# Merge tile 0 prepared inside the delta stage, logits moved inside a projection, expert gathers moved behind a stage border

## The chip, the cores and the metric

One core of one Trainium2 chip. The metric is the device time of one execution in microseconds. Engines are named as in the profile: PE (TensorE matmul), DVE (VectorE), ACT (ScalarE), POOL (GpSimd), SP (SyncE, which here only issues DMAs). Each engine runs its own list of instructions in order and waits on semaphores for the others.

## The reference

One layer of a bidirectional encoder over 1024 sample tokens and 256 prompt tokens, D = 1024, all in float32:

```python
x += W_out( sig(gA) * W_pA(GatedDeltaNet_bidir(n)) + sig(gB) * W_pB(DilatedWindowAttn(n)) )   # n = RMSNorm(x)
x += ExpertChoiceSwiGLU(RMSNorm(x))
# merge of the mixer, per token:
oa = rmsnorm(o_fwd + o_bwd, a_norm) * silu(z)              # 8 heads of 64
ya = oa @ w_proj_a
weights = softmax(stack(lses)); ob = sum(weights * outs)   # 3 dilation groups, 4 heads
yb = ob @ w_proj_b
x = x + (sigmoid(gate_a) * ya + sigmoid(gate_b) * yb) @ w_out
# routing: every expert takes its best tokens (128 of the sample, 32 of the prompt)
aff = softmax(rmsnorm(x) @ w_router); gate, idx = top_k(aff.T, cap)
ye = (silu(x[idx] @ w_gate) * (x[idx] @ w_up)) @ w_down * gate     # added back at idx; 16 experts
```

## The kernel before

The layer is a chain of stages, each a Block in which all five engines run their lists. A Block ends when every engine has drained; then the stage's semaphores are cleared and a second barrier lets the next stage begin (signals, L48).

phase_delta (L1419) walks 20 chunks of 64 tokens (STEPS), 16 of the sample and 4 of the prompt. Both directions go side by side: the backward half of step s works on the last chunk not yet done, so that tokens 0 to 127 are complete once the sample's 16 steps are stored. In each step PE solves and carries, ACT copies u and w (L1638, L1639), then the state and the outputs (L1641, L1644), DVE masks and carries (L1655 to L1675), POOL prepares later steps (L1498 to L1505). SP loads step s and stores step s-3; at step 16 it also issues the mixer's weights (load_mixer, L1725: w_proj_a, w_proj_b and w_out in two halves) into the buffer "weights", whose eight slots later hold expert weights (HELD = 8).

phase_merge (L1770) takes 10 tiles of 128 tokens (8 sample, 2 prompt). For a tile POOL adds the two directions, squares, scales and multiplies by silu(z) (L1894 to L1904); DVE sums the squares and prepares the softmax over the three groups (statistics, L2110) and mixes them (weighted, L2122, result mg_ob); ACT does Silu, Sigmoid, Ln, Exp with a table load at each change (L2062 to L2073). PE turns the two inputs (turn_in), projects them in two column halves (project_in, 12 matmuls each), DVE multiplies with the gates (gated, L2096), PE turns the mix (turn_mix), projects it (project_out, 16 records per half), DVE adds x (residual), ACT finds the root (L2053 to L2057), DVE scales (normed), PE turns and finds the logits (turn_normed, logits), ACT and DVE make affinities, PE turns them (turn_affinities), DVE keeps them (take_affinities). The tiles are staggered by a hand-written order over c = 0 .. 14: PE in iteration c does project_in of tile c-2, turn_mix and project_out of c-3, turn_normed and logits of c-4, turn_affinities of c-5, turn_in of c-1 (L1988 to L2013).

Routing ranks affinities eight at a time on DVE, 16 rounds over the 640 tokens of tiles 0 to 4 (low_best), 16 over the rest (high_best, 384 wide; the last four rounds also rank the prompt). A fixed number of rounds is placed between the other work: LOW_AT_ONCE (L1745) inside the loop over c, and the list from L2234 behind it. The two lists are merged, PE turns the indices, DVE writes them to the tensors of Routing (L1748), and POOL gathers the first inputs of the experts (L1905 to L1909) before the Block ends. keep_busy (L562) issues matmuls with the identity whose results nobody reads.

phase_experts (L2302) turns the gathered rows, splits them in a rounded part and a rest, and multiplies 12 weight pieces per expert for 16 experts: multiply(e, n).

## Time and profile before

| | us |
|---|---|
| median of three runs (2550.56 to 2558.72) | 2550.92 |
| profiled execution | 2563.21 |
| its span, first to last instruction | 2561.5 |
| last delta matmul ends | 1321.9 |
| merge's first load is issued | 1327.33 |
| first merge transpose | 1353.47 |
| merge's Block ends | 1681.5 |
| first expert product | 1695.31 |
| mean granted clock of TensorE, share of full speed | 0.966 |

Times inside the execution are microseconds from the start of the span. The profile is of one execution, so sums are made against 2563.21.

### The profile page before, as it was taken

How to read it: one execution, taken by the hardware profiler on the slowest of the kernel's cores; microseconds unless marked ns; L12 is line 12 of the kernel's file. 1: busy time of each engine (PE TensorE's matmuls, PEld its weight loads, DVE VectorE, ACT ScalarE, POOL GpSimd, SP SyncE). 2: the span in 40 equal slices, each digit the busy share in tenths (PEclk: the TensorE clock that was granted, in tenths of full speed). 3: DMA queues.
4: the chain of work that ended last, by engine and by line, in shares of the span. 5: the costliest groups of instructions: out<-in, count | busy, mean ns of one | idle time of the engine just before them, and what ended most of it. 6: DMA issues, size and time to landing. Idle time of an engine off the chain costs nothing. (4 is left out here: it accounts for less than half of the span.)

```text
span 2561.5 us, 49483 instructions
## 1 busy us (share of the span) xinstructions
PE 2366.1 (92%) x20746; PEld 2117.0 (83%) x20746; DVE 1389.6 (54%) x1774; ACT 1079.3 (42%) x1605; POOL 394.4 (15%) x411
## 2 busy tenths in 40 slices
PE   6988899889999999988868999979999999999996
PEld 5766688889999988988853555579999999999996
DVE  5544411134444367332226456867777777777776
ACT  4555511111111068111126553246666666666664
POOL 1000000000000094644313220000000100010001
PEclk8999999999999999998988999989999999999998
DMA  3333432238666377444644441448777877777765
GB/s 118 76 86 86 108 117 95 97 102 264 184 203 185 131 216 220 129 127 122 216 123 149 134 139 55 184 173 282 267 248 274 269 264 274 263 261 263 274 233 195
DMA packets 174174, 461.30 MB, mean 180 GB/s; under 512 B 57361, under 2 KB 103057, under 8 KB 146353
## 3 DMA queue, kind: packets, MB, share of 16 engines
q1 hardware_dynamic: 160944, 412.63, 49.2%
q0 software_dynamic: 13024, 45.70, 6.2%
q8 instruction: 158, 2.59, 0.4%
q14 instruction: 48, 0.39, 0.0%
HBM read 359.94 MB, written 102.24 MB: 180 GB/s over the span
## 5 line engine op out<-in xcount | busy, mean ns | idle before, releaser
L78 DVE TENSOR_TENSOR ex_w_rest<-weights,ex_w_rounded 128x2048 fp32r<-128x2048 f32 x192 | 439.5, 2290 | 209.8 <-ACT ex_w_rounded L2531 208.0
L2531 ACT CAST ex_w_rounded<-weights 128x2048 fp32r<-128x2048 f32 x192 | 365.6, 1905 | 25.9 <-PEq L48 25.9
L2422 PE MATMUL ex_u_acc<-ex_xt,ex_w_rounded 128*128 128x320 f32 x1024 | 271.7, 348 | 0.0
L2422 PE MATMUL ex_g_acc<-ex_xt,ex_w_rounded 128*128 128x320 f32 x1024 | 270.1, 347 | 1.6 <-issue 1.6
L85 PE MATMUL tk_acc<-tk_w_rounded,normed 128*128 128x336 f32 x800 | 257.3, 322 | 6.8 <-DVE tk_w_rest L78 6.8
L85 PE MATMUL tk_acc<-tk_w_rounded,normed_rest 128*128 128x336 f32 x800 | 255.0, 319 | 0.0
L85 PE MATMUL tk_acc<-tk_w_rest,normed 128*128 128x336 f32 x800 | 254.6, 318 | 0.0
L2423 PE MATMUL ex_u_acc<-ex_xt,ex_w_rest 128*128 128x160 f32 x1024 | 242.1, 236 | 0.0
L2423 PE MATMUL ex_g_acc<-ex_xt,ex_w_rest 128*128 128x160 f32 x1024 | 242.0, 236 | 0.0
L2423 PEld LDWEIGHTS ex_u_acc<-ex_xt,ex_w_rest 128*128 128x128 f32 x1024 | 196.4, 192 | 0.0
L2423 PEld LDWEIGHTS ex_g_acc<-ex_xt,ex_w_rest 128*128 128x128 f32 x1024 | 196.3, 192 | 0.0
L2422 PEld LDWEIGHTS ex_g_acc<-ex_xt,ex_w_rounded 128*128 128x128 f32 x1024 | 192.9, 188 | 1.8 <-issue 1.8
L2422 PEld LDWEIGHTS ex_u_acc<-ex_xt,ex_w_rounded 128*128 128x128 f32 x1024 | 193.0, 189 | 0.2
L85 PEld LDWEIGHTS tk_acc<-tk_w_rounded,normed 128*128 128x128 f32 x800 | 152.0, 190 | 10.5 <-DVE tk_w_rest L78 7.0
L85 PE MATMUL ch_wide<-normed,ch_w_rounded 128*128 128x512 f32 x384 | 152.0, 396 | 5.2 <-DMA ch_headsum<-in_headsum 5.2
L1177 DVE COPY tk_stage<-tk_acc 128x336 f32<-128x336 f32 x50 | 25.4, 508 | 241.8 <-PE tk_acc L85 241.8
L1116 ACT COPY tk_stage<-tk_acc 128x336 f32<-128x336 f32 x50 | 21.8, 437 | 313.8 <-PE tk_acc L85 313.8
L85 PEld LDWEIGHTS tk_acc<-tk_w_rest,normed 128*128 128x128 f32 x800 | 152.1, 190 | 0.0
L85 PEld LDWEIGHTS tk_acc<-tk_w_rounded,normed_rest 128*128 128x128 f32 x800 | 151.5, 189 | 0.0
L85 PE MATMUL ch_wide<-normed_rest,ch_w_rounded 128*128 128x512 f32 x384 | 150.7, 392 | 0.0
L85 PE MATMUL ch_wide<-normed,ch_w_rest 128*128 128x512 f32 x384 | 150.6, 392 | 0.0
L1945 PE MATMUL mg_out<-weights,mg_mix_t 128*128 128x512 f32 x320 | 141.4, 595 | 0.3 <-ACT mg_mix_t L2041 0.3
(342 smaller groups left out, 5239.4 us busy)
## 6 DMA issues: line engine op xcount, KB each, us to landing
weights<-in_w_expert SPq DMA_DIRECT2D x192, 1024.0 KB, 5.0
laq<-sc_laq SPq DMA_DIRECT2D x20, 768.0 KB, 4.0
dl_la<-laq SPq DMA_DIRECT2D x20, 768.0 KB, 5.2
proj_tok<-tk_stage SPq DMA_DIRECT2D x9, 1680.0 KB, 7.8
tk_w<-in_w_tok SPq DMA_DIRECT2D x10, 1344.0 KB, 6.8
ch_w<-in_w_ch SPq DMA_DIRECT2D x24, 512.0 KB, 4.1
sc_rows<-rows SPq DMA_DIRECT2D x40, 256.0 KB, 6.5
sc_qk<-qkv_ch SPq DMA_DIRECT2D x40, 256.0 KB, 6.8
```

Of the source, the lines that this page charges most:

```text
L78: return dve.tensor_tensor(out, whole, rounded.bitcast(F32), ALU.subtract)
L85: mm = pe.matmul(out, stationary[a], moving[b], start=(first and n == 0), stop=(last and n == len(pairs) - 1))
L1116: act.copy(stage[:, c % 2, t, :], acc[:, n % BANKS, 0:TOK_BLOCK]).then_inc(copied[0], 1)
L1177: dve.tensor_copy(stage[:, c % 2, t, :], acc[:, n % BANKS, 0:TOK_BLOCK]).then_inc(copied[1], 1)
L1945: mm = pe.matmul(out[:, h, :], mix_t[:, k, :], wo[k // 4][:, k % 4, h * 512:(h + 1) * 512], start=(k == 0), stop=(k == KT - 1))
L2422: pe.matmul(bank[:, 0:2 * SLOTS], hi[:, cols], x.rearrange("p a n -> p (a n)"), start=first, stop=False, skip_group_check=True)
L2423: return pe.matmul(bank[:, 0:SLOTS], lo[:, cols], x[:, 0, :], start=False, stop=last, skip_group_check=True)
L2531: act.copy(w_hi[:, i % SPLIT], held[:, i % HELD]).then_inc(w_rounded, 1)
```

## The change

- A class FirstTile holds tile 0 of the merge. It is loaded by SP in the delta stage, before the store of step 16, into slots 3, 6 and 7 of "weights". POOL's sums and scale, ACT's Silu, roots and Sigmoid, DVE's statistics and weighted of tile 0 stand in the delta stage's lists around the last step; PE gets 16 keep_busy matmuls at its end.
- The second half of w_out, which had slots 6 and 7, is loaded at the start of the merge behind tile 1's inputs, under a semaphore of its own (rest_ready), on which project_out(0, 0) waits. MIXER_WEIGHTS is 3.
- The merge's engines count up tile 0's semaphores (sem_inc) and start with tile 1. The constants are loaded at c = 1; nobody waits for them at the start.
- PE's order for the first tiles is written out, and so is the iteration of the last sample tile.
- DVE's ranking rounds and tail are placed anew; the last tile's turned mix goes to a free gates buffer.
- The two first gathers are issued by POOL at the start of the expert stage; the sample's comes first there, and the prompt's turn writes to y_acc. BUSY_RANKS is 16 instead of 30, BUSY_GATHER 12 instead of 20.

```diff
@@ phase_delta, SP
+                    if isinstance(s, int) and s == STEPS - 1:
+                        for r in range(2):
+                            sp.wait_ge(stored[r], 32 * S_STEPS // 2)
+                        first_tile.load(sp, io, dr)
@@ phase_delta, POOL, PE, ACT, DVE
                 ring_steps(pool, prepare)
+                first_tile.sums(pool)
+                first_tile.scale(pool)
                 ring_steps(pe, step)
+                keep_busy(pe, ybank[:, 0, 0:P], ident, 16)
                 def step(s, b, i, prompt):
+                    if isinstance(s, int) and s == STEPS - 1:
+                        first_tile.activate(act)
                     act.wait_ge(uw_done, s + 1)
...
                     act.copy(paired(wb[:]), uw[:, :, :, 1, :]).then_inc(uw_out, 1)
+                    if isinstance(s, int) and s == STEPS - 1:
+                        first_tile.roots(act)
...
                 ring_steps(act, step)
+                first_tile.open_gates(act)
...
+                    else:
+                        first_tile.statistics(dve)
                     carried(s, b)
...
                 ring_steps(dve, step)
+                first_tile.weighted(dve)
@@ FirstTile (new; six loads on one semaphore)
+    def load(self, sp, io, dr):
+        rows = slice(0, P)
+        for d in range(2):
+            sp.dma_start(self.od[:, d], dr["o_delta"][d, rows, :]).then_inc(self.loaded, 16)
+        sp.dma_start(self.z, dr["proj_tok"][rows, Z_AT:Z_AT + HEADS * HD]).then_inc(self.loaded, 16)
+        sp.dma_start(self.att.rearrange("p g c -> p (g c)"), dr["att_out"][rows, :]).then_inc(self.loaded, 16)
+        sp.dma_start(self.gates, dr["proj_tok"][rows, GATE_AT:GATE_AT + 2 * D]).then_inc(self.loaded, 16)
+        sp.dma_start(self.again[:], io["a_norm"].partition_broadcast(P)).then_inc(self.loaded, 16)
+    def sums(self, pool):       # add the directions, square
+    def scale(self, pool):      # times rstd, a_norm, silu(z); waits rstd, then silu
+    def activate(self, act):    # waits loaded; Silu of z
+    def roots(self, act):       # waits mean, eps; Ln, Exp; waits dm; Exp
+    def open_gates(self, act):  # Sigmoid of the gates
+    def statistics(self, dve):  # waits squared; head sums, maxima
+    def weighted(self, dve):    # waits exp; weights, three products, reduction to ob
@@ phase_merge, SP
-                load(0)
-                for dst, src in ((again...), (fgain...), (wr...)):
-                    sp.dma_start(dst, src).then_inc(S["const"], 16)
+                sp.sem_inc(inputs[0], 64)
+                sp.sem_inc(gates_in[0], 16)
+                load(1)
+                load_rest(sp)
                 for c in range(NT + LAST):
-                    if has(c + 1):
+                    if c >= 1 and has(c + 1):
                         load(c + 1)
+                    if c == 1:
+                        for dst, src in ((fgain...), (wr...)):
+                            sp.dma_start(dst, src).then_inc(S["const"], 16)
@@ phase_merge, POOL
-                for b in range(2):
-                    pool.wait_ge(hn_stored[b], 16 * NT // 2)
-                pool.wait_ge(S["handed"], 2)
-                routing.gather_prompt(pool, dr, 0)
-                routing.gather(pool, dr, 0)
@@ phase_merge, PE
-                for c in range(NT + LAST):
+                turn_in(0)
+                project_in(0, 0)
+                project_in(0, 1)
+                turn_mix(0)
+                project_out(0, 0)
+                turn_in(1)
+                project_out(0, 1)
+                project_in(1, 0)
+                project_in(1, 1)
+                turn_in(2)
+                for c in range(4, NT + LAST):
...
+                    if c - 4 == LAST_SAMPLE:
+                        turn_normed(c - 4)
+                        project_out(c - 3, 0, range(KT // 2))
+                        pe.wait_ge(S["aff_taken"], c - 4)
+                        logits(c - 4)
+                        project_out(c - 3, 0, range(KT // 2, KT))
+                        turn_affinities(c - 4)
+                        turn_mix(c - 2)
+                        project_out(c - 3, 1)
+                        continue
@@ phase_merge, ACT: turned_out(0) first; in c = 1 after the roots of tile 1
+                    if c == 1:
+                        mix_out(0)
+                        open_gates(1)
@@ phase_merge, DVE
-LOW_AT_ONCE = {9: (0, 1, 2), 10: (1, 2, 3), 11: (1, 2, 3)}
+LOW_AT_ONCE = {9: (0, 0, 1, 2), 10: (1, 1, 2, 3)}      # the first number stands between highest and normed
+                gated(0, 0)
+                gated(0, 1)
+                for c in range(1, NT + 1):                # gated(c - 2) only from c = 3
...
+                highest(LAST_SAMPLE - 1)
+                low_best(1)
+                normed(LAST_SAMPLE)
+                affinities(LAST_SAMPLE - 1)
+                gated(NT - 1, 0)
+                low_best(1)
+                gated(NT - 1, 1)
+                take_affinities(LAST_SAMPLE - 1)
+                low_best(2)
+                highest(LAST_SAMPLE)
+                affinities(LAST_SAMPLE)
+                low_best(1)
+                take_affinities(LAST_SAMPLE)
+                residual(NT - 2, 0)
+                high_best(3)
+                residual(NT - 2, 1)
                 high_best(2)
                 normed(NT - 2)
+                residual(NT - 1, 0)
                 low_best(ROUNDS - low_rounds[0])
-                residual(NT - 1, 0)
                 high_best(4)
                 residual(NT - 1, 1)
                 high_best(1)
                 highest(NT - 2)
                 normed(NT - 1)
                 affinities(NT - 2)
+                high_best(2)
                 take_affinities(NT - 2)
-                high_best(1)
                 highest(NT - 1)
-                high_best(1)
                 affinities(NT - 1)
@@ phase_experts
+                gather(0)            # POOL, first in its list
+                gather_prompt(0)
                 keep_busy(pe, g_acc[:, 0, 0:P], ident, BUSY_GATHER)
+                turn_in(0)
                 turn_in_prompt(0)
-                pe.wait_ge(xpt_lo, 2)
-                turn_in(0)
@@ ACT and DVE of phase_experts: round_x(0), rest_x(0) stand before the prompt's
```

## Rows read from the trace of the kernel before

**Rows 1.** The page, part 1: busy time, share of the span, instructions.
```profile
PE 2366.1 (92%) x20746; PEld 2117.0 (83%) x20746; DVE 1389.6 (54%) x1774; ACT 1079.3 (42%) x1605; POOL 394.4 (15%) x411
```

**Rows 2.** Waits, 1321 to 1358: who <- whom: total us, times, longest.
```profile
PE mg_in_turned L1964 <- DVE mg_ob L2139: 31.5, 1, 31.5
POOL mg_on L1894 <- DMA mg_wr<-in_w_router: 11.7, 1, 11.7
```

**Rows 3.** Timeline of PE: start, us, instructions [idle before <-releaser].
```profile
1356.74 5.76 PE L1923 MATMUL mg_y<-weights,mg_mixin_t 128*128 128x512 f32 x8 [1.76 <-ACT mg_mixin_t L2084]
...
1370.91 3.70 PE L1923 MATMUL mg_y<-weights,mg_mixin_t 128*128 128x512 f32 x8 [0.89 <-ACT mg_mixin_t L2084]
...
1376.16 1.04 PE L1936 MATMUL mg_wide_turned<-identity,mg_mix 128*128 128x128 f32 x8
...
1382.81 7.03 PE L1945 MATMUL mg_out<-weights,mg_mix_t 128*128 128x512 f32 x16
...
1397.20 3.60 PE L1923 MATMUL mg_y<-weights,mg_mixin_t 128*128 128x512 f32 x8
...
1404.37 3.70 PE L1923 MATMUL mg_y<-weights,mg_mixin_t 128*128 128x512 f32 x8 [0.99 <-DVE mg_mix L2103]
...
1426.59 3.68 PE L1923 MATMUL mg_y<-weights,mg_mixin_t 128*128 128x512 f32 x8
```

**Rows 4.** Timelines of ACT and DVE at the merge's start.
```profile
1334.83 1.28 ACT L2065 ACT_TABLE_LOAD   x1 [11.76 <-DMA mg_att<-att_out]
...
1341.40 1.91 ACT L2067 ACTIVATE mg_gates<-mg_gates 128x2048 f32<-128x2048 f32 x1
...
1348.98 3.27 DVE L2134 TENSOR_TENSOR mg_wv<-mg_att,mg_st 128x256 f32<-128x256 f32 x3
...
1373.76 1.94 DVE L2134 TENSOR_TENSOR mg_wv<-mg_att,mg_st 128x256 f32<-128x256 f32 x3
```

**Rows 5.** Timeline of DVE at the merge's end.
```profile
1637.21 0.54 DVE L2199 MAX8 mg_high_val<-mg_high_aff 16x8 f32<-16x384 f32 x1
...
1644.32 0.69 DVE L2149 TENSOR_TENSOR mg_x<-mg_out,mg_x 128x512 f32<-128x512 f32 x1
...
1653.92 0.28 DVE L2179 COPY mg_high_aff<-mg_in_turned 16x128 f32<-16x128 f32 x1 [4.23 <-PE mg_in_turned L1983]
...
1664.31 0.55 DVE L2199 MAX8 mg_high_val<-mg_high_aff 48x8 f32<-48x384 f32 x1
```

**Rows 6.** Drains at the merge's end (ns, start); the prompt gather's landing.
```profile
L1836 DVEq DRAIN  x1: 415/415/415, 1673.6 to 1673.6; - x1
L1836 POOLq DRAIN  x1: 6634/6634/6634, 1674.9 to 1674.9; - x1
...
DMA to landing us min/median/max: 4.3/4.3/4.3
```

**Rows 7.** Timeline of PE at the expert stage's start; one window behind it.
```profile
1682.63 7.54 PE L562 MATMUL ex_g_acc<-identity 128*128 128x128 f32 x40 [9.10 <-PEq L48]
...
1695.31 0.50 PE L2422 MATMUL ex_g_acc<-ex_xt,ex_w_rounded 128*128 128x320 f32 x1 [1.61 <-issue]
...
1700.00:1750.00 50.00, 50.00 (x393) 50.00 (x392) 38.27 (x36) 33.27 (x36) 2.20 (x2) 1.00 0.81 298
```

**Rows 8.** Timelines of ACT and DVE, from x2 to the scaled tile.
```profile
1598.36 1.06 ACT L2053 ACTIVATE mg_sqx<-mg_x 128x1024 f32<-128x1024 f32 x1 [6.61 <-DVE mg_x L2149]
...
1602.67 1.29 DVE L2157 SCALAR_TENSOR_TENSOR mg_hn<-mg_x,mg_st,mg_fgain 128x1024 f32<-128x1024 f32 x1 [3.05 <-ACT mg_st L2057]
```

**Rows 9.** DMA queues, 1326 to 1345.
```profile
DMA packets 2769, 5.11 MB, mean 269 GB/s; under 512 B 1360, under 2 KB 1360, under 8 KB 2512
```

**Rows 10.** Delta steps: waits of PE 1236 to 1280; ACT's copy of u.
```profile
PE dl_sbank L1602 <- issue: 3.0, 2, 1.6
...
1266.54 0.58 ACT L1638 COPY dl_u<-dl_ubank 128x512 f32<-128x512 f32 x1 [6.55 <-PE dl_ubank L1526]
...
1315.12 0.58 ACT L1638 COPY dl_u<-dl_ubank 128x512 f32<-128x512 f32 x1 [2.62 <-PE dl_ubank L1526]
```

More of the change, by code:

```diff
@@ L1712 @@
 HALF = 512
-MIXER_WEIGHTS = 4
+MIXER_WEIGHTS = 3
 def shared_weights(nc, ctx, io):
@@ L1726, in load_mixer, with load_mixer_rest @@
         rows = lambda w: w.rearrange("(k p) c -> p k c", p=P)
-        for dst, src in ((mixer[0], rows(io["w_proj_a"])), (mixer[1], rows(io["w_proj_b"])),
-                         (mixer[2][0], rows(io["w_out"])[:, 0:4]), (mixer[2][1], rows(io["w_out"])[:, 4:])):
+        for dst, src in ((mixer[0], rows(io["w_proj_a"])), (mixer[1], rows(io["w_proj_b"])), (mixer[2][0], rows(io["w_out"])[:, 0:4])):
             engine.dma_start(dst, src).then_inc(mixer_ready, 16)
+    def load_mixer_rest(engine):
+        engine.dma_start(mixer[2][1], io["w_out"].rearrange("(k p) c -> p k c", p=P)[:, 4:]).then_inc(mixer_rest_ready, 16)
     def load_expert(engine, pieces):
@@ L1821, in phase_merge @@
         listed, prompt_listed = y[:, 0, :], out[:, 0, :]
+        last_mix_t = gates[:, (NT - 3) % 3, 0:D].rearrange("p (k n) -> p k n", k=KT)
+        gate = lambda t: gates[:, t % 3] if t else first_tile.gates
+        mixes_t = lambda t: last_mix_t if t == NT - 1 else mix_t
         S = {n: sem(f"mg_{n}") for n in (
@@ L1937, in turn_mix, with project_out @@
                     mm.then_inc(S["mix_turned"], 1)
-                def project_out(t, h):
+                def project_out(t, h, ks=range(KT)):
                     if h == 0:
@@ L1943, in project_out @@
                         pe.wait_ge(S["x2"], 2 * (t - 1) + h + 1)
-                    for k in range(KT):
-                        mm = pe.matmul(out[:, h, :], mix_t[:, k, :], wo[k // 4][:, k % 4, h * 512:(h + 1) * 512], start=(k == 0), stop=(k == KT - 1))
-                    mm.then_inc(S["out_done"], 1)
+                    else:
+                        pe.wait_ge(rest_ready, 16)
+                    for k in ks:
+                        mm = pe.matmul(out[:, h, :], mixes_t(t)[:, k, :], wo[k // 4][:, k % 4, h * 512:(h + 1) * 512], start=(k == 0), stop=(k == KT - 1))
+                    if ks.stop == KT:
+                        mm.then_inc(S["out_done"], 1)
                 def turn_normed(t):
                     pe.wait_ge(S["hn"], t + 1)
-                    pe.wait_ge(S["mix_t"], min(t + 2, NT))
+                    pe.wait_ge(S["mix_t"], min(t + 2, NT) if t != NT - 2 else NT)
                     for k in range(KT):
@@ L1972, in logits @@
                         pe.wait_ge(S["lexp"], t)
+                    else:
+                        pe.wait_ge(S["const"], 32)
                     pe.wait_ge(S["on_t"], min(t + 4, NT))
@@ L2215, in _ @@
                         affinities(c - 5)
-                    if has(c - 2):
+                    if has(c - 2) and c > 2:
                         gated(c - 2, 0)
@@ L2220, in _ @@
                     low_best(low_a)
-                    if has(c - 2):
+                    if has(c - 2) and c > 2:
                         gated(c - 2, 1)
@@ L2549, in round_prompt @@
                             act.wait_ge(xt_prompt, GANG * g)
-                        act.copy(xpt[:, 4 * half:4 * half + 4, 0, :], turned[:, half].rearrange("p (k n) -> p k n", k=4)).then_inc(xpt_hi, 1)
+                        act.copy(xpt[:, 4 * half:4 * half + 4, 0, :], prompts_turned(g)[:, half].rearrange("p (k n) -> p k n", k=4)).then_inc(xpt_hi, 1)
                 def gate_half(e, j):
@@ L2670, in rest_prompt @@
                         here = xpt[:, 4 * half:4 * half + 4]
-                        rest(dve, here[:, :, 1, :], turned[:, half].rearrange("p (k n) -> p k n", k=4), here[:, :, 0, :]).then_inc(xpt_lo, 1)
+                        rest(dve, here[:, :, 1, :], prompts_turned(g)[:, half].rearrange("p (k n) -> p k n", k=4), here[:, :, 0, :]).then_inc(xpt_lo, 1)
                 def gate_sum(e, j):
```

257 lines of the change are left out of this document (164 added, 93 removed).

## The prediction

> **What bounds the kernel now.** I read the page first: TensorE (PE) is busy for 92% of the span [rows 1], so time can come only from stretches in which PE waits, or from work taken off the path. Three such stretches lie where the diff works.
>
> First, the list of waits around the border of the delta rule and the merge: PE waits 31.5 us for the first tile's attention mix, mg_ob [rows 2]. In order of time: the last delta matmul ends at 1321.9 and the merge's first loads are issued at 1327.33 (both in the table); ScalarE (ACT) is released by the inputs' landing at 1334.83, the first add on GpSimd (POOL) waits 11.7 us for the router weights, and the first transpose comes 31.5 us after the last delta matmul, at 1353.47 [rows 2, 4].
>
> Second, the end of the merge. From tile 3 on (project_in at 1426.59 [rows 3]) PE runs on without a gap, so there only its own work counts. Then the ranking on VectorE (DVE) is what is late: it idles 4.23 us for the turned affinities at 1653.92, and its last four rounds start only at 1664.31 [rows 5].
>
> Third, the entry of the expert stage: POOL's drain at the merge's end takes 6634 ns, from 1674.9 to 1681.5, while DVE's took 415 ns at 1673.6; PE then starts at 1682.63, fills 7.54 us with 20 keep_busy matmuls, turns two inputs from about 1690, and multiplies from 1695.31 [rows 6, 7]. After that PE is full to the end (50.00 of 50 us, clock 1.00) [rows 7], so what is gained before 1695.31 is gained in the total.
>
> **Part 1: the merge starts with tile 0 prepared.** I write times on the old axis. Inside the delta stage: POOL has done its last preparation at 1295, so the sum and square of tile 0 (1.3 + 1.0 us) cost nothing; ACT loads a table and does Silu in the 2.6 us before the last step's copies; the two root tables and DVE's 1.4 us of statistics fit into waits of 5.8 and 5.2 us. After the last carry (1319.5) DVE has 1.0+0.2+0.2+0.9, three products (3.27 us beside POOL, 1.94 alone [rows 4]) and a 1.0 reduction: done at 1325.5 to 1326.3. ACT's Sigmoid of the gates follows the last output copy at 1323.1: table 1.28 + 1.91 [rows 4] = 1326.3. The last stores end the stage at 1326.2 now, so I put the stage's end 0.9 later and the first transpose at 1328.2.
>
> From there I walk PE's new order with the old pitches [rows 3]: a copy gap 0.9, project_in pairs 10.5 (2 x 5.25, from 1370.91 to 1376.16), mixed 1.8 later, turn 0.9, project_out half 6.9 (7.03 with its overlap). Up to turn_mix(0) this gives 1343.3. But ACT must first finish tile 1's roots, whose sums DVE takes only after gated(0,1) at 1342.2; 0.7 + 0.3 + table 1.28 + 0.4 bring the copy of the mix to 1345.0 and project_out(0,0) to 1346.1. Then: half 1353.0, turn 1353.7, half 1360.6, project_in of tile 1 1371.1, turn 1371.8, project_in(2,0) 1372.7. Old was 1397.20, so 24.5 us so far.
>
> There a new wait comes. project_in(2,1) needs gated(2,0), and DVE comes to it only after gated(1,1) (1372.7), weighted(3) (6.2 us beside POOL), two residual halves (1.3), the ACT chain from x2 to the root (1598.36 to the scaling at 1602.67, 4.3 [rows 8]), that scaling (1.3) and the product (0.6): 1386.6. Old was 1404.37 [rows 3]: 17.8 us are left, PE idle 7.6. Such an idle stretch costs clock: after the old one 8 matmuls took 5.76 us at the 1.2 GHz level against 3.70 later [rows 3], 2.1 us; with the smaller gaps before it I take off 3.3. **Part 1: 14.5 us.** Bounds: 24.5 if the chain is not late; 8 if w_out's second half, now loaded after the border, is late too. That load: 4.34 MB stand in the queue up to its end, and the queue moved 5.11 MB at 269 GB/s from 1326 to 1345 [rows 9], so it lands near 1342, 4 us before 1346.1. Queued behind it on SP are tile 2's inputs and the constants, which nobody wants before 1351.
>
> Moves inside the delta stage: 2 MB fewer of mixer weights at 1236, 2.2 MB of tile 0 more at about 1285. With the DMA full, steps stretched: at 1266.54 ACT waited 6.55 us for PE's solve, at 1315.12, undisturbed, 2.62, and PE itself had waits that the profile explains by nothing, 3.0 us in the largest group [rows 10]. Call it 7 to 10 us for the burst of 7 MB, 1.2 us per MB (an estimate from these rows): 2.5 saved, 2.6 paid. I take 0, bounds -5 and +4.
>
> The Trainium skill (Runtime: NRT & Kernel Launch, Instruction fetch mechanics) says that sequential fetch is mostly hidden. By that rule both terms would be nil and the sum the same; the rows speak against it while the DMA is full [rows 10].
>
> **Part 2: the merge's tail.** PE's order is changed (logits of tile 7 inside project_out of tile 8, turn_mix(9) earlier, tile 9's mix in its own buffer), the sum of its work is not; the 0.7 us of gaps at 1628 goes. DVE: three waits of some 3 us take one low round each (2.55). The price: between the residual halves of tile 9 stand now 1 low + 4 high rounds, 2.55 + 7.1 (1637.21 to 1644.32, four rounds and little else [rows 5]) from 1636.0, so the second half comes at 1645.7 instead of 1644.32, 1.3 late, and the norm, turn and logits of tile 9 with it. The gain: all 12 high rounds that need no prompt are done before the turned affinities at about 1655.2, where 7 were, and two of them fill the 4.23 us. What follows is take 0.3, highest 0.3, exponent and affinities 1.3, turn 0.5, take 0.3: the last four rounds start at 1657.8 instead of 1664.31. **Part 2: 6.5 us**, bounds 3 (another slip of the chain through tile 9) and 8 (none). The cut of the keep_busy matmuls (30 to 16) lies beside the four rounds of 7 us and cost nothing unless the clock falls.
>
> **Part 3: gathers after the border.** Before, POOL issued both gathers at the merge's end and its drain held all engines until they had landed [rows 6]: the overlap with the border was none. Now DVE's drain ends it: 1674.0 + 1.1 (1681.5 to 1682.6, as old) = 1675.1. Sample gather from there: 0.9 issue, landed about 5 us after its start, 1680.2 (prompt gather's landing 4.3 us [rows 6]); the prompt's 1.3 later, 1681.6. PE's 12 keep_busy matmuls end by 1679.8. Turn 1.0, prompt turn ending 1682.6, then round, rest and take: 3.3 after the prompt's turn starts, 1685.0 (old: 5.1 from the first turn to the product, the second turn and its round between). Old 1695.31 [rows 7]. **Part 3: 10.3 us**; bounds 12.5 and 6 (a gather that lands 4 us later, beside the first expert weights).
>
> A second rule stands beside parts 1 and 3. The trace has three products at 3.27 us while POOL runs and 1.94 when it does not [rows 4]. The Trainium skill (SBUF — State Buffer, SBUF: two separate sides) calls the port pair of VectorE and GpSimd an exclusive lock for instructions with two SBUF inputs. By it weighted beside POOL's scale ends up to 1.3 us later, which moves the stage's end by less than 1.
>
> Sum: 14.5 + 0 + 6.5 + 10.3 = 31. The profiled execution took 2563.2 us (span 2561.5 and 1.7 around it), so it would be 2532; the median of the runs is 2550.9, 12.3 lower, and I take the same 31 off it: **2520 us**.
>
> **Rivals.**
> (A) *No late chain at the start.* If gated(2,0) is reached in time, because PE's own gaps pull apart less than I walked, part 1 is 24.5 less 1: 2511. For it: old, DVE was only 0.99 us late at this very place; against it: the residuals stand behind weighted(3) in DVE's list, and po(0,1) is now 12 us earlier relative to them without helping.
> (B) *Early loads are paid in delta steps.* Tile 0's 2.2 MB meet steps 17 and 18, and each loses what the half step at 1266 lost, 3.9 us [rows 10], one of them twice that; the saving at 1236 does not come back. With 8 paid, 23: 2528.
> (C) *Gathers or chain slips.* Part 3 gives 6, part 2 gives 3: 2527 or 2528.
> (D) *The other side: w_out's second half.* PE's project_out(0,0) waits for it and everything queues behind. Up to 1346.1 it is free; from there each us costs one. With the 31 us it decides from a landing at 1377. The 4.34 MB would need 87 GB/s, and 8 MB with tile 2's inputs shared in would need 160; the queue gave 269. At 1386 it would give 2560.
> (E) *The change does not do what it says*: tile 0's loads wait for sample stores and land after 1313, so ACT holds the last delta step for them; the gap moves into the stage. Stores of step 15 are issued at 1277.7, 35 us earlier. It would leave parts 2 and 3 alone: 2534.
>
> **How the numbers follow.** Forecast 57%, A 13%, B 11%, C 11%, D 3%, E 5%. The range takes A and C and most of B and E: 2508 to 2535. A measurement of this kernel tells 0.3% (7.7 us) from no change. Faster needs more than 7.7 of the 31: 95%; same 3%, slower 2%, both from D and from tails of B and E together.
>
> **What would show it.** Right: first merge transpose 5 to 7 us after the last delta matmul; POOL's drain at the merge's end under 1 us; a PE wait of 5 to 9 us before project_in(2,1), released by DVE's mix product, and none after it; the last four ranking rounds 6 to 7 us sooner after tile 9's project_in; first expert product about 11 us after DVE's last index copy instead of 21.3. Wrong: PE waiting for a DMA before project_out(0,0), delta steps over 14 us after the loads, or a gather that PE waits for beyond 7 us.

## The result, and the profile after

The changed kernel takes **2534.4 us** (median of 7 runs, 2521.8 to 2538.2); the kernel before took 2558.7 us in its 7 runs of the same comparison (2550.6 to 2569.3). Ratio 0.9908, 95% interval 0.9885 to 0.9930: **24 us faster, between 18 and 29**. The forecast was 31 us, 1.2% of 2550.9. Its sign held, and its range (2508 to 2535) by 0.6 us; the size did not: 1.2% lies outside the interval. Of the 14 us between 2520 and 2534, 7.8 come from the median it started from (2550.9 in three runs, 2558.7 in seven), the rest from the gain.

The profiled execution of the changed kernel happens to be its fastest, 2521.8 us (span 2520.1); 41 us lie between the two profiles, far more than between the medians. So the comparison needs a point that the change can't move. I take ScalarE's last copy of u in the delta rule (1315.12 before [rows 10], 1300.27 after) and count from there; what lies ahead of it is a section of its own below.

| from the last copy of u, us | before | after | gain | forecast |
|---|---|---|---|---|
| to project_in(3,0) (part 1) | 111.47 | 98.53 | 12.9 | 14.5 |
| from there to project_in(9,0) (steady) | 172.48 | 172.47 | 0 | 0 |
| from there to the last four rounds (part 2) | 65.24 | 58.04 | 7.2 | 6.5 |
| from there to the last index copy's end | 9.67 | 9.67 | 0 | 0 |
| from there to the first expert product (part 3) | 21.33 | 15.63 | 5.7 | 10.3 |
| to the first product in all | 380.2 | 354.3 | 25.9 | 31.3 |
| from the first product to the end | 866.2 | 865.5 | 0.7 | 0 |

The delta steps in front of that point cost about 1.2 us more (below, a mean that scatters by over 1 us), which leaves 24.7 of 25.9, near the measured 24. Busy time answers to [rows 1]; PE has 19 us less, in an execution with a mean granted clock of 0.979 against 0.966:

```profile
PE 2347.0 (93%) x20734; PEld 2101.8 (83%) x20734; DVE 1388.1 (55%) x1774; ACT 1079.6 (43%) x1605; POOL 395.2 (16%) x411
```

**Part 1.** The timeline of PE at the merge's start (start, us, instructions, idle before and its releaser), which answers to [rows 2, 3]:

```profile
1313.30 0.63 PE L2071 MATMUL mg_in_turned<-identity,ft_on 128*128 128x128 f32 x4 [2.44 <-DVEq L2228]
...
1315.04 5.22 PE L2027 MATMUL mg_y<-weights,mg_mixin_t 128*128 128x512 f32 x8 [0.89 <-ACT mg_mixin_t L2180]
...
1332.28 8.56 PE L2051 MATMUL mg_out<-weights,mg_mix_t 128*128 128x512 f32 x16 [2.48 <-ACT mg_mix_t L2170]
...
1373.65 6.62 PE L2027 MATMUL mg_y<-weights,mg_mixin_t 128*128 128x512 f32 x8 [7.15 <-DVE mg_mix L2242]
...
1398.80 3.68 PE L2027 MATMUL mg_y<-weights,mg_mixin_t 128*128 128x512 f32 x8
```

The 31.5 us wait is gone: the first transpose comes 6.2 us after the last delta matmul (end at 1307.1; forecast 6.3). The late chain is there as well: PE idles 7.15 us before project_in(2,1) (forecast 7.6), released by VectorE's mix product, and VectorE shows why, since that product stands behind the scaling of tile 0, which waited 4.34 us for ScalarE's root:

```profile
1371.71 1.28 DVE L2298 SCALAR_TENSOR_TENSOR mg_hn<-mg_x,ft_st,mg_fgain 128x1024 f32<-128x1024 f32 x1 [4.34 <-ACT ft_st L2194]
1372.91 0.68 DVE L2242 TENSOR_TENSOR mg_mix<-mg_y,mg_gates 128x512 f32<-128x512 f32 x1
```

What the forecast had too small is the clock: behind each of the three idle stretches (2.44 + 0.89 us around the first turns, 1.58 + 2.48 around the turn of the mix, 7.15) PE's matmuls are slow, 5.22 instead of 3.65 us, 8.56 instead of 7.03 and 6.62 instead of 3.60. That is 6.1 us where 3.3 were taken off. The price of one stretch is not fixed: in the second profile of the same kernel (below) the three groups took 6.65, 8.83 and 5.51 us behind the same waits.

**Part 2.** VectorE at the merge's end [rows 5]: the wait for the turned affinities (second line) is 0.92 us instead of 4.23.

```profile
1617.30 0.69 DVE L2288 TENSOR_TENSOR mg_x<-mg_out,mg_x 128x512 f32<-128x512 f32 x1
...
1626.97 0.28 DVE L2322 COPY mg_high_aff<-mg_in_turned 16x128 f32<-16x128 f32 x1 [0.92 <-PE mg_in_turned L2092]
...
1629.31 0.55 DVE L2342 MAX8 mg_high_val<-mg_high_aff 48x8 f32<-48x384 f32 x1
```

**Part 3.** The drain that took 6634 ns [rows 6] lies now in the middle of the merge (GpSimd's at 1531.9, 1644 ns where under 1 us was forecast; nothing waits for it there); VectorE's ends the stage at 1639.0, and PE starts at 1640.11. Up to there all is as forecast. Then, on the axis of the changed kernel, one timeline per engine:

```profile
1640.81 1.06 POOL L2547 DMA_INDIRECT ex_xs<-hn,rt_sample_idx  x1 [107.33 <-POOLq L48]
1642.18 2.96 POOL L2552 DMA_INDIRECT ex_xp<-hn,rt_gang_idx  x1 [0.30 <-issue]
...
1642.01 2.29 DVE L78 TENSOR_TENSOR ex_w_rest<-weights,ex_w_rounded 128x2048 fp32r<-128x2048 f32 x1 [3.03 <-ACT ex_w_rounded L2694]
...
1644.33 0.33 SPq L2529 DMA_DIRECT2D weights<-in_w_expert  x1
...
1645.36 1.29 PE L2631 MATMUL ex_turned<-identity,ex_xs 128*128 128x128 f32 x8
1650.50 1.97 PE L2639 MATMUL ex_y_acc<-identity,ex_xp 128*128 128x128 f32 x8 [3.86 <-DMA ex_xp<-hn,rt_gang_idx]
1654.61 0.60 PE L2586 MATMUL ex_g_acc<-ex_xt,ex_w_rounded 128*128 128x320 f32 x1 [2.14 <-ACT ex_xt L2706]
```

Read the second gather first: 2.96 us on GpSimd, where both gathers of the kernel before took about 1.0. It is the only one beside which VectorE works on a product with two large inputs in SBUF (the first weight rest, what is left of a weight after rounding); that product began 0.17 us before the gather and ended 0.84 us before the gather did. When that product is done SyncE sends the first weight load (1 MB) off, still ahead of the gather's data. The next gather, at 1646.91, ran beside VectorE's rests of the turned rows, which have one input in PSUM, and took 0.94 us. The prompt is turned 11.5 us after the index copy (forecast 7.6), and the products start at the low clock: the last slow one ends 20.6 us after the copy.

### The profile page after: what moved, and what is told of

Same layout as the page of the kernel before. It is cut to its first block and busy times, and to the rows that moved or that the text cites. A ratio compares the mean times of both kernels' runs of the same rounds, so it can differ in the third digit from the quotient of the medians.

```text
span 2520.1 us, 49483 instructions
## 1 busy us (share of the span) xinstructions
PE 2347.0 (93%) x20734; PEld 2101.8 (83%) x20734; DVE 1388.1 (55%) x1774; ACT 1079.6 (43%) x1605; POOL 395.2 (16%) x411
## 5 line engine op out<-in xcount | busy, mean ns | idle before, releaser
L2586 PE MATMUL ex_y_acc<-ex_ht,ex_w_rounded 128*128 128x320 f32 x512 | 135.1, 347 | 0.2 <-DVE ex_ht L78 0.2
```

The source lines that it names most:

```text
L2586: pe.matmul(bank[:, 0:2 * SLOTS], hi[:, cols], x.rearrange("p a n -> p (a n)"), start=first, stop=False, skip_group_check=True)
```

## The experiments

Times below count from the last copy of u, or, at the expert stage's entry, from the end of the last index copy. The totals are against the kernel before on the same chip.

**Undo one part, or do one alone.** The kernel before with part 3 alone (the expert stage and the gathers from the changed kernel, its 12 keep_busy matmuls):

> Kernel before with part 3 alone: gathers issued in the expert stage, sample first, 12 instead of 20 keep_busy matmuls, turns and rounds in the changed kernel's order. Theory (part 3 is worth what the trace of the changed kernel shows, 5.7 us, and not the 10.3 forecast): from VectorE's last index copy to the first product 15 to 16 us instead of 21.3; total 0.2% less. Rival (the forecast's size was right and the changed kernel's entry was a bad draw): 11 to 12 us, total 0.4% less.

Measured: 2556.4 us, ratio 0.9986 (0.9970 to 1.0002). First product at 15.78, second gather 2.96 us, prompt turned at 11.67. The theory holds for the stretch: part 3 is worth 5.6 us of it by itself, with the same late prompt, so not a bad draw and not a consequence of parts 1 and 2. The total alone would not tell it from nothing.

Two things the 5.6 us hide. The old entry scatters too: in the next run, which leaves it as it was, the first product comes at 19.92 instead of 21.33, so the gain lies between 4.1 and 5.6 us. And in the old entry PE turned the first input right behind its 20 keep_busy matmuls, which took 7.54 us in one profile [rows 7] and 6.21 in the other, though the prompt's gather had landed at 1679.0, 4.3 us after its start [rows 6]:

```profile
1690.01 1.04 PE L2475 MATMUL ex_turned<-identity,rt_xp 128*128 128x128 f32 x8
```

```profile
1675.37 6.21 PE L562 MATMUL ex_g_acc<-identity 128*128 128x128 f32 x40 [9.03 <-PEq L48]
```

So a part of the gain is the cut from 20 to 12 keep_busy matmuls: 8 of 20 are 2.5 to 3.0 us, an estimate from these two groups. No run makes that cut alone.

The kernel before with the second half of w_out loaded at the merge's start:

> Kernel before with one part of the change alone: the second half of w_out (2 MB) is loaded at the merge's start, behind the inputs of tiles 0 and 1, not in the delta rule. Theory of the forecast (2.5 us of stretched delta steps saved): from the copy of step 14 to that of step 19 65 to 66 us instead of 67.4 to 68.2; the rest unchanged, from the last delta copy to the end 1241 to 1246 us. Rival 1 (those steps are not stretched by the load): 67 to 68. Rival 2 (the load at the border delays what the merge's start needs): first merge transpose later than 38.4 us after the last delta copy.

Measured: step 14 to step 19 took 67.1 us, against 68.2 and 67.4 in the two other kernels with the old delta rule; first transpose at 37.6. Rival 1 holds: 2 MB fewer there give nothing that stands out of the scatter. Nor does the load hurt at the border. In the eleven profiles with the new delta rule the same five steps took 67.1 to 70.1, mean 68.8 against 67.6 before; the step after tile 0's loads is 1.5 to 2.0 us longer in ten of them and 0.7 in one, and PE shows a wait of "issue" in it, that is for nothing that the profile shows (waits of PE, 1274.8 to 1288.3 of the changed kernel), while from 1272 to 1276 the DMA engines were full (share 1.03, 407 GB/s):

```profile
PE dl_sbank L1556 <- issue: 1.3, 1, 1.3
```

What PE waited for there no run shows.

Logits of tile 7 behind the whole half of project_out instead of inside it:

```diff
-                        project_out(c - 3, 0, range(KT // 2))
+                        project_out(c - 3, 0)
                         pe.wait_ge(S["aff_taken"], c - 4)
                         logits(c - 4)
-                        project_out(c - 3, 0, range(KT // 2, KT))
```

> Changed kernel with the logits of tile 7 after the whole half of project_out(8,0) instead of inside it. From project_in(9,0) to the last four ranking rounds it is 58.04 us in the changed kernel. Theory (VectorE is full between tile 7's logits and those rounds but for waits of 1.5 and 1.0 us, so logits 3.4 us later come through in part): 59 to 60 us. Rival (the ranks are bound elsewhere, by the residual of tile 9 and its norm chain): 58.0 us, and the move inside is worth nothing.

Measured: 62.33 us instead of 58.04. More than the 3.4 us of the move came through (4.3), so my theory's damping by 1.5 and 1.0 us of waits was wrong; the order inside the projection carries 4.3 of part 2's 7.2 us.

**The late chain.** In VectorE's order at the merge's start:

```diff
+                    if c == 3:
+                        residual(0, 0)
+                        residual(0, 1)
+                        gated(2, 0)
                     if has(c):
                         weighted(c)
```

(and all three left out where they stood)

> Changed kernel with VectorE's order altered at the merge's start only: the residual halves of tile 0 and the mix product gated(2,0) come ahead of weighted(3). Theory (the 7.15 us wait before project_in(2,1) is VectorE's order, and the 6.62 us instead of 3.60 after it is the clock paid for that wait): the wait goes (under 0.5 us), project_in(2,1) takes 3.6 to 3.7 us, and from the merge's first load to project_in(3,0) it is 76 to 77 us instead of 86.4; total about 10 us less than the changed kernel. Rival 1 (the wait moves on: project_out(1,0) or the turning of hn(0) waits for ScalarE's roots instead): 3 to 7 us of it come back in the next 20 us. Rival 2 (the slow matmuls come from the stage's start, not from this wait): the wait goes but project_in(2,1) stays above 5 us.

Measured: 2519.3 us, ratio 0.9849 (0.9827 to 0.9872); project_in(3,0) at 89.79 instead of 98.53 to 99.2 (77.7 from the merge's first load, expected 76 to 77). PE has no wait between turn_mix(1) and project_in(2,1) any more, and the matmuls behind run at full speed:

```profile
1372.81 1.04 PE L2040 MATMUL mg_wide_turned<-identity,mg_mix 128*128 128x128 f32 x8
1373.68 3.60 PE L2027 MATMUL mg_y<-weights,mg_mixin_t 128*128 128x512 f32 x8
```

Theory confirmed, rival 1 and rival 2 both gone: the wait was an order in a list, and 3.0 us behind it were its price in clock.

**The clock at the start.** On top of that kernel: 32 keep_busy matmuls after the delta rule, 6 before project_out(0,0), and ScalarE's copy of mix(0) ahead of tile 1's roots:

```diff
-                keep_busy(pe, ybank[:, 0, 0:P], ident, 16)
+                keep_busy(pe, ybank[:, 0, 0:P], ident, 32)
...
                 turn_mix(0)
+                keep_busy(pe, out[:, 0, 0:P], ident, 6)
                 project_out(0, 0)
```

> The kernel with gated(2,0) ahead, and at the merge's start: 32 instead of 16 keep_busy matmuls at the end of the delta rule, ScalarE's copy of mix(0) ahead of tile 1's roots, 6 keep_busy matmuls between turn_mix(0) and project_out(0,0). Counted from ScalarE's last dl_u copy, that kernel had the first transpose at 13.0 us, project_in(0,0) for 6.12 us from 15.2, project_out(0,0) for 8.83 us from 33.3 and project_in(3,0) at 89.8. Theory (PE's short waits cost clock, and the copy stands behind roots that nobody needs so early): project_in(0,0) 3.6 to 4.5 us, project_out(0,0) from 30.5 for 7.0 us, project_in(3,0) at 84 to 85, 5 us less in total. Rival 1 (the low clock comes from the border's idle itself, not from a short one): project_in(0,0) stays above 5 us, 3 us less in total. Rival 2 (tile 1's roots, now 1 us later, hold turn_in(1) and the copy of its sums): project_out(0,1) and project_in(1,0) a microsecond later, gain of the copy given back.

Measured: 2527.4 us, ratio 0.9867 (0.9829 to 0.9906); project_in(3,0) at 89.93, nothing gained. Two things took the gain:

```profile
1319.56 7.41 PE L562 MATMUL dl_ybank<-identity 128*128 128x128 f32 x64
...
1328.83 0.63 PE L2071 MATMUL mg_in_turned<-identity,ft_on 128*128 128x128 f32 x4 [1.86 <-DVEq L2230]
...
1330.57 3.70 PE L2027 MATMUL mg_y<-weights,mg_mixin_t 128*128 128x512 f32 x8 [0.89 <-ACT mg_mixin_t L2181]
...
1348.13 1.01 DVE L2270 TENSOR_TENSOR mg_st<-mg_st,mg_att 128x12 f32<-128x12 f32 x1 [4.27 <-ACT mg_st L2213]
...
1353.80 1.03 DVE L2280 TENSOR_REDUCE mg_ob<-mg_wv 128x256 f32<-128x768 f32 x1
...
1354.93 0.63 PE L2071 MATMUL mg_in_turned<-identity,mg_on 128*128 128x128 f32 x4 [2.89 <-issue]
```

The clock is right (3.70 us, where the kernel without the fillers had 6.12, and project_out(0,0) 7.06 instead of 8.83), but 32 matmuls take 7.41 us, end after everything else in the stage, and hold its end: first transpose at 16.0 instead of 13.0, so turn_mix(0) starts at 29.91 instead of 29.77. The changed kernel's 16 (3.84 us) do not hold the end.

The second is rival 2, larger than it said. With the copy of mix(0) ahead of them, tile 1's roots come behind the copy and a table load, and VectorE waits 4.27 us for them instead of 1.52. Its chain for tile 1 ends with mg_ob at 1354.83, and turn_in(1), which needs mg_ob, starts 0.1 us later: at 42.12, where the kernel without fillers had 42.01. The 2.9 us that project_out(0,0) had gained by then are PE's wait of 2.89. The profile calls it "issue", but it is the wait for mg_ob.

**The expert stage's entry.** VectorE's first weight rest moved behind the sample's rests:

```diff
-                split_weights(0)
                 rest_x(0)
+                split_weights(0)
                 rest_prompt(0)
```

> Changed kernel with one edit: VectorE's first weight rest, which ran from 1642.01 for 2.29 us beside GpSimd's prompt gather (2.96 us on GpSimd instead of 1.06), now follows the sample columns' rests. Theory (the two products block GpSimd's descriptor work through the shared port): the prompt gather takes 1.0 to 1.2 us on GpSimd, its data are turned 1.9 us sooner after VectorE's last index copy (11.5 us before, 9.6 now), and the first expert product comes at 13.7 us after that copy's end instead of 15.6. Rival (the gather itself is slow, because it is the second of two or because its list of rows is four times as scattered): 2.96 us and 15.6 us stay. Total against the changed kernel: 2 us less, below what a ratio of totals can tell.

Measured: 2526.1 us, ratio 0.9879 (0.9861 to 0.9897). The gather takes 0.96 us, and the prompt is turned at 8.35 instead of 11.5:

```profile
1650.04 0.96 POOL L2552 DMA_INDIRECT ex_xp<-hn,rt_gang_idx  x1 [0.31 <-issue]
...
1655.19 1.09 PE L2639 MATMUL ex_y_acc<-identity,ex_xp 128*128 128x128 f32 x8 [0.68 <-DMA ex_xp<-hn,rt_gang_idx]
1660.21 0.61 PE L2586 MATMUL ex_g_acc<-ex_xt,ex_w_rounded 128*128 128x320 f32 x1 [3.93 <-ACT ex_xt L2706]
```

The rival (slow because second) is out. But 3.2 us were gained at the prompt and not 1.9, and only 2.3 at the product (13.37), since the rest now stands between the prompt's turn and its rests. The 3.2 have a second cause, and the weight load was the candidate. Changed kernel, the first weight load alone held until the prompt's turn:

```diff
+                sp.wait_ge(xp_turned, 2)
                 for i in range(HELD, NP * EXPERTS):
```

> Changed kernel with one wait more: the expert stage's first weight load (1 MB, issued at 1644.33, before the prompt gather was issued to its end at 1645.14) waits for the prompt's turn. In the kernels with that overlap the prompt was turned 5.3 to 5.5 us after GpSimd had done its gather instruction, without it 4.2. Theory (the load delays the gather's landing): gather instruction 2.96 us as before, prompt turned 10.3 to 10.4 us after the last index copy instead of 11.5. Rival (the 1.2 us come from VectorE or from the memory's state and not from the load): 11.4 to 11.6.

Measured: gather 2.96 us as before, prompt turned at 9.51, first product at 12.91.

```profile
1650.91 2.96 POOL L2553 DMA_INDIRECT ex_xp<-hn,rt_gang_idx  x1 [0.30 <-issue]
...
1657.22 1.09 PE L2640 MATMUL ex_y_acc<-identity,ex_xp 128*128 128x128 f32 x8 [2.12 <-DMA ex_xp<-hn,rt_gang_idx]
```

From the end of GpSimd's instruction to the turn it is 3.35 us, in the changed kernel 5.36: the load costs the gather 2.0 us, more than the 1.2 I expected. Then the suspected cost doubled, VectorE's product done twice back to back:

```diff
+                dve.wait_ge(w_rounded, 1)
+                rest(dve, w_lo[:, 1], held[:, 0], w_hi[:, 0]).then_inc(extra, 1)
                 split_weights(0)
+                dve.wait_ge(extra, 1)
```

> Changed kernel with the suspected cost doubled: VectorE's first weight rest (2.29 us) is done twice, back to back, the first time into a slot that is written anew later. Theory 1 (GpSimd gets through only when VectorE is idle): the prompt gather takes 2.96 + 2.29 = 5.2 us on GpSimd, the weight load goes out 2.3 us later too, and the prompt is turned 13.5 to 14 us after the last index copy. Theory 2 (GpSimd waits out the one instruction that it meets, and takes the port between two): the gather stays at 2.9 to 3.3 us, VectorE's second product is late or longer instead, and the weight load, 2.3 us later, no longer goes ahead of the gather: prompt turned at 9.5 to 10.5 us. Rival (the port has no part in it): the gather 2.96 us, the second product 2.29 us and right behind the first.

```profile
1640.88 2.96 POOL L2553 DMA_INDIRECT ex_xp<-hn,rt_gang_idx  x1 [0.31 <-issue]
...
1640.72 4.49 DVE L78 TENSOR_TENSOR ex_w_rest<-weights,ex_w_rounded 128x2048 fp32r<-128x2048 f32 x2 [3.03 <-ACT ex_w_rounded L2695]
...
1645.24 0.33 SPq L2530 DMA_DIRECT2D weights<-in_w_expert  x1
...
1647.17 1.63 PE L2640 MATMUL ex_y_acc<-identity,ex_xp 128*128 128x128 f32 x8 [2.02 <-DMA ex_xp<-hn,rt_gang_idx]
```

Theory 2 holds for the gather: 2.96 us again, so GpSimd waits out the one instruction that it meets: it was done 0.87 us after the first product's end, while the second ran. Its guess that the second product would be late or longer fell: the two take 4.49 us, 2.25 each. And the useless product makes the kernel faster at this place, first product at 13.25 instead of 15.6, because it sends the weight load 2.2 us later: from the end of GpSimd's instruction to the turn it is 3.3 us, as with the load held.

Two rearrangements more. First the later rest with 10 keep_busy matmuls between the turns and 8 behind them:

> As the kernel with the later weight rest, and 10 keep_busy matmuls between the sample's turn and the prompt's turn and 8 after it, in waits of PE. Theory (the 4.8 us of slow products after the first product are paid for PE's waits of 3.9 and 2.1 us ahead of them): the first products run at 0.35 us a pair's first matmul instead of 0.55, which gives 2 us at most, and the fillers cost under 0.5 us. Rival (fillers at the low clock take 0.45 us each, 4.5 us for ten, and hold the prompt's turn up): first product later by 1 to 3 us than without them. Against the changed kernel in total: 2 to 4 us less by the theory, 0 to 2 less by the rival.

Measured: 2527.6 us, ratio 0.9878 (0.9853 to 0.9902). First product at 13.08 (13.37 without), all products at full speed, where without fillers they are slow up to 16.8; and yet from the first product to the end 866.7 us in both. The ten fillers do hold the prompt's turn up, as the rival said (9.45 instead of 8.35), but it was not what the product waited for, since VectorE's weight rest stands behind it. In all the fillers bring 0.3. With a warm start PE waits for the next pieces' rests instead (0.5 us for VectorE's sum, and 0.7 us idle in the first 20), as a warm PE is ahead of VectorE's 2.29 us per piece. Second, prompt gather first, and the rest to wait for both gathers:

> Changed kernel with the expert stage's entry rearranged: the prompt gather is issued first, VectorE's first weight rest waits until GpSimd has issued both gathers, the first expert weight load waits for the sample's turn, turns and rounds follow in the order prompt, sample, and 2 and 6 keep_busy matmuls stand in PE's waits. Theory (of the 15.6 us from VectorE's last index copy to the first product 1.9 are the two products' hold on GpSimd, 1.2 the first weight load beside the prompt gather's landing, 0.7 slow turns): both gathers 1.0 us each on GpSimd, prompt turned at 7.0 us after the copy, sample at 8.3, first product at 10.8 to 11.5, at the full clock, rest to the end 866 us or up to 1.2 more. Rival (a gather's landing takes what it takes, and with VectorE held back the rests are what is late): first product at 13 us or later, as in the run with the later weight rest (13.4).

Measured: 2530.4 us, ratio 0.9883 (0.9845 to 0.9922). First product at 12.37, between theory and rival, and the gather issued second is slow again: 3.04 us, now the sample's. VectorE's product started at 1653.27, 0.09 us before that gather: GpSimd's count, which stands behind both gathers in its list, had risen before the second began. VectorE was not held back, so the run shows once more which two instructions meet and says nothing on the rival.

**All of it together**, and the changed kernel again beside it. The delay of VectorE's rest is now done with ScalarE's table load:

```diff
+                keep_busy(pe, out[:, 0, 0:P], ident, 4)
                 turn_in(0)
+                keep_busy(pe, out[:, 0, 0:P], ident, 3)
                 project_in(0, 0)
...
+                act.activation(ss[:, 0, 0:1], ident[:, 0:1], ACT.Silu)
                 round_weights(0)
+                round_prompt(0)
                 round_x(0)
```

> Changed kernel with what the runs so far favour: gated(2,0) and tile 0's residual ahead of weighted(3); the copy of mix(0) ahead of tile 1's roots; the end of the delta rule as in the changed kernel, but 4, 3 and 7 keep_busy matmuls in PE's waits before turn_in(0), project_in(0,0) and project_out(0,0); and at the expert stage's entry the prompt gather first, a Silu on one column (its table load, 1.28 us) ahead of ScalarE's first weight rounding, so that VectorE's first weight rest starts after both gathers are issued, the first weight load after the sample's turn, 2 and 6 keep_busy matmuls in the waits. Theory (these waits are in line one behind another, so what is saved adds up): from the last dl_u copy 84 to 87.5 us to project_in(3,0) (98.5 in the changed kernel), both gathers 1.0 us on GpSimd, first product 10.3 us after the last index copy (15.6), from the last dl_u copy to the end 1203 to 1206 us (1219.8); 0.6% less than the changed kernel in total. Rival (the entry's gain is given back, since after an early first product PE waits for the next pieces' rests): first product at 10.3 but 1 to 2 us more behind it. Rival (fillers at the low clock delay what they stand before): first transpose over 13.5 us after the last dl_u copy.

> The changed kernel itself once more, beside the kernel with all additions, for two comparisons: its total against that kernel's on the same chip, and a second profile. Theory (all spread of the total lies ahead of the change): the start of the delta rule's first step differs from 1036.0 by some us, and from the last dl_u copy to the end it is 1219.8 us within 0.7. Rival (the parts that the change touches scatter as well): that stretch differs by over 2 us.

Measured: **2520.1 us for all together, ratio to the kernel before 0.9842 (0.9812 to 0.9871)**, and 2536.3 us for the changed kernel (0.9913, 0.9887 to 0.9939): 16 us between their medians on one chip. To the first product it is 340.5 us, in the changed kernel 354.3 and 355.1.

```profile
1327.57 3.70 PE L2027 MATMUL mg_y<-weights,mg_mixin_t 128*128 128x512 f32 x8 [0.22 <-ACT mg_mixin_t L2183]
...
1342.21 7.03 PE L2051 MATMUL mg_out<-weights,mg_mix_t 128*128 128x512 f32 x16
1350.81 1.03 DVE L2282 TENSOR_REDUCE mg_ob<-mg_wv 128x256 f32<-128x768 f32 x1
...
1351.95 0.63 PE L2071 MATMUL mg_in_turned<-identity,mg_on 128*128 128x128 f32 x4 [2.70 <-issue]
...
1352.63 8.73 PE L2051 MATMUL mg_out<-weights,mg_mix_t 128*128 128x512 f32 x16
...
1643.89 1.06 POOL L2563 DMA_INDIRECT ex_xp<-hn,rt_gang_idx  x1 [107.75 <-POOLq L48]
1645.25 0.96 POOL L2558 DMA_INDIRECT ex_xs<-hn,rt_sample_idx  x1 [0.30 <-issue]
...
1646.46 2.29 DVE L78 TENSOR_TENSOR ex_w_rest<-weights,ex_w_rounded 128x2048 fp32r<-128x2048 f32 x1 [4.41 <-ACT ex_w_rounded L2707]
...
1653.32 0.38 PE L2597 MATMUL ex_g_acc<-ex_xt,ex_w_rounded 128*128 128x320 f32 x1 [0.27 <-DVE ex_xt L78]
```

The fillers hold the clock up to project_out(0,0), the first transpose stays at 13.0, both gathers take 1.0 us, and the first product comes at 11.27 (expected 10.3). At the start it is 88.65 (expected 84 to 87.5): project_out(0,0) comes 2.6 us sooner, but turn_in(1) waits 2.70 us for mg_ob of tile 1, as in the run with 32 fillers and for the same reason (ScalarE's copy of mix(0) ahead of tile 1's roots), and project_out(0,1) behind it runs 8.73 us instead of 7.03. Without these 4.4 us the expectation would have held (84.3, an estimate from these rows).

From the first product to the end both kernels took longer than in any other profile, 869.7 and 869.9 us against 864.9 to 866.8: so the rival of the second expectation holds too, that stretch can scatter by 4 us. It is not the entry's gain given back, since the changed kernel shows it as well. In all 14 profiles PE waits 1.63 to 1.65 us, three times in the expert stage, before a turn (about 193, 403 and 613 us behind the first product). In these two profiles the clock falls behind the second and the third of these waits; in the other twelve the products behind all three run at full speed. The kernel with all additions, and the first profile of the changed kernel at the same wait:

```profile
2055.82 1.93 PE L2642 MATMUL ex_turned<-identity,ex_xs 128*128 128x128 f32 x8 [1.63 <-DVE ex_xpt L78]
...
2056.00:2059.00 3.00, 3.00 (x15) 3.00 (x15) 0.90 (x3) 1.80 (x4) 0.98 (x1) 0.50 0.88 350
```

```profile
2055.00:2065.00 10.00, 8.36 (x67) 8.17 (x66) 7.98 (x10) 6.47 (x10) 1.01 (x1) 1.00 0.74 264
```

A granted clock of 0.50 for 3 us, the 1.2 GHz level, against 1.00. Each such fall costs 1.6 us. A later wait of 2.40 us (at about 801 us) is followed by slow products in these two and in four others, and by none in the other eight. What decides it no run shows.

## Where the 41 us between the two profiles lie

The first step's copy of u came at 1048.97 us before and at 1036.02 after, 13 us apart, though nothing ahead of it was changed; the second profile of the changed kernel had 1048.18, and all 14 profiles lie between 1036 and 1053. Two stages make it up: the channel projections (their last wide matmul started at 446.7 in this profile of the changed kernel, at 455.4 in that of the kernel before and at 448.6 to 454.9 in the other twelve) and the attention (from the last token matmul to the delta rule's first product for u 149 to 160 us). From the last copy to the first product, in contrast, the changed kernel's two profiles agree within 0.8 us, and the steady stretch is 172.47 or 172.48 in all 14. So 41.4 = 13.0 ahead of the first step, 1.9 in the delta steps (scatter of that stage, 259 to 267 us over all profiles), 25.9 to the first product and 0.7 behind it. Why the early stages scatter was not looked into.

## Why the prediction was right and where it failed

- *The border and the prepared tile*: right. First transpose 6.2 us after the last delta matmul; the stage's end did not even move by the 0.9 us allowed; the preparation hides in the delta steps but for 1.2 us.
- *The late chain* (7.6 us forecast, 7.15 found): right, and shown by taking it away. Rival A is dead.
- *The clock in part 1*: **wrong in size**. "With the smaller gaps before it I take off 3.3" should have been 6.1; three idle stretches of 3.3, 4.1 and 7.2 us cost 1.6, 1.5 and 3.0 (3.0, 1.8 and 1.9 in the second profile), while the 31.5 us before had cost 2.1: short ones were not cheaper. My walk of the gaps was 1.2 us too long, so the term came out 1.6 too high.
- *Delta moves*: forecast 2.5 saved and 2.6 paid. Paid: 1.5 to 2.0 in the step after the loads, seen as a wait of "issue" (1.3 in the changed kernel's profile). Saved: nothing measurable. The sum, 0, was 1.2 us too good.
- *The tail*: right (6.5, found 7.2), and over half of it is the logits' place.
- **The failed step is part 3's "the prompt's 1.3 later, 1681.6"**, the prompt gather's landing, 7.6 us after the last copy. It was 11.5. I took both gathers' costs from a stretch in which VectorE and the queue of SyncE were idle, and moved them to one where both are busy. Two mechanisms follow: VectorE's product holds GpSimd (1.9 us in the instruction), and the weight load that this product releases goes off ahead of the gather's data and delays them (2.0 us); without both it is 8.35 and not 7.6, since behind a gather issued sooner 4.19 us pass instead of 3.35. Of the 4.6 us by which part 3 fell short these are 3.9; the other 0.7 lie behind the prompt's turn, which itself ran slow (1.97 us instead of 1.04). Rival C had the price of part 3 right (6, the weights named) but half the mechanism, and that its total (23 us) comes near the measured 24 is luck: its other half, a part 2 of 3 us, did not happen, and parts 1 and the delta steps lost what it left alone. The Trainium skill (SBUF — State Buffer, SBUF: two separate sides) has the other half: it warns that a DMA issued by GpSimd starves while VectorE holds the shared port pair. I had used the section for the three products of weighted, and not for the gathers. The trace agrees on the block (2.96 us against 0.96). What it adds: with two products back to back the gather was held by the first alone, and the second (2.25 us) did not grow while the gather went on beside it. That the port pair is what the two share is the page's account; the runs show which instructions meet and what it costs.

## What to carry to other kernels

When an operation moves into another stage, its duration does not come along: ask what runs beside it there, on the engine that shares its port and in the queues that share its DMA engines. TensorE's waits of 3 to 7 us cost another 1.5 to 3 us in clock each here, so look for the list order behind one before filling it; and when an item is moved ahead in a list, look for who waits for what it was moved ahead of: ScalarE's copy came 1.1 to 1.3 us sooner, and PE waited 2.7 to 2.9 us at the next turn. A filler is free only up to the moment at which its stage would end anyway, and when fewer fillers go in together with another edit, their share has to be measured by itself. And compare two profiles from a fixed point that the change can't move: here 13 us of the 41 between them belonged to no edit.

## What was not expected of the hardware

- An indirect gather on GpSimd takes 1.0 us alone and 2.96 to 3.04 beside one VectorE product of 128x2048 with two SBUF inputs that started 0.1 to 0.2 us earlier; still 2.96 beside two of them back to back.
- A 1 MB load sent off 0.8 us before a gather's instruction ended moved the gather's use from 3.35 to 5.36 us behind that end.
- A semaphore increment that stands behind two gathers in GpSimd's list released VectorE 0.09 us before the second gather started.
- Behind one and the same wait of PE (1.63 to 1.65 us) the products ran on at full speed in 12 of 14 profiles; in 2 the granted clock fell to 0.50 for about 3 us, which cost 1.6 us each time.
- VectorE's products with one input in PSUM did not slow a gather that ran beside them: 0.94 us.
